# Gate columns of a fused decoder layer: two products per chunk instead of three, an added half on VectorE, softmax weights scaled on ScalarE

## The chip, the cores and the metric

One core of one Trainium2 chip. The time is the device time of one execution in microseconds; before the change it is 456.95 us, the median of three runs (456.88 to 457.21). Lower is better.

## The reference, cut to what matters

One decoder layer on 256 tokens of 1024 features, all in float32. A first half mixes tokens, a second half is a SwiGLU. The mixer, on its modulated and normalised input `h`:

```python
proj = h @ w_in                                   # 256 x 6504
(q_sb, k_sb, v_sb, q_mb, k_mb, v_mb, q_ds, k_ds, v_ds,
 q_ix, k_ix, w_ix, gate_logits) = jnp.split(proj, ...)
o_sb = stick_breaking_attention(q_sb, k_sb, v_sb)     # 6 heads, no softmax
o_mb = moba_attention(q_mb, k_mb, v_mb, slopes)       # 5 heads, softmax
o_ds = dsa_attention(q_ds, k_ds, v_ds, ...)           # 5 heads, softmax over 64 picked keys
g_sb, g_mb, g_ds = jnp.split(jax.nn.sigmoid(gate_logits + b_gate), 3, axis=-1)
merged = g_sb * (o_sb @ w_proj_sb) + g_mb * (o_mb @ w_proj_moba) + g_ds * (o_ds @ w_proj_dsa)
y = merged @ w_o
```

The 3 x 1024 columns of `gate_logits` are what the change touches, and beside them the division of the softmax weights by their sum in the ten softmax heads.

## The kernel before, in words

**Numbers in two parts.** A float32 operand of a matrix product is cut into a high part (`whi`, `hhi`) and the rest (`wlo`, `hlo`). ScalarE makes the high part by a copy (`cut_hi`, L749), VectorE the rest by a subtraction (`cut_lo`, L1113). TensorE then adds three products, high x high, high x low and low x high, in one PSUM bank (`three`, L1579 to L1581). The two parts of `h` lie side by side in `hcut` (128 partitions, 8 chunks, 2 parts, 256 tokens), so the two parts of a chunk are also one operand of 512 columns. The SwiGLU's first product already uses that (`up`, L1982 and L1983): one product of 512 columns with `whi`, which puts high x high in the first half of a bank and high x low in the second, and one of 256 columns with `wlo`, added to the second half.

**Units.** The product with `w_in` is made in 51 units, numbered 0 to 50, of up to 128 features for all tokens (or up to 384 features for 128 tokens). Weights come in blocks of up to 512 columns. The last 24 units, 27 to 50 (`FIRST_GATE` = 27), are the gate columns, four units to a block (blocks 11 to 16). Two banks take turns; `unit(u)` on TensorE (L1677) waits until the bank of unit u-2 has been read, and `take_unit(u)` on ScalarE (L800, gates in L829) reads it: it adds the bias and writes to `gates`, which has `qk`'s place, so the trace calls it qk. Up to unit 45 L829 adds the bias alone, and from 46 (`SIGMOID_FROM`) it makes the sigmoid too; in the passes of units 46 to 49 four larger instructions (L968) make the sigmoid of the 19 tiles before.

**One order for all engines.** Every engine runs through a pass for each u, and tables say what else a pass holds: `PIECES_AT` the cuts of the next block (a quarter each in the gate passes, two in the first pass of block 16), `SCORES_AT`, `EXP_AT`, `NORM_AT` and `SECOND_AT` the four steps of an attention head (head n begins in pass 14+2n, its steps in successive passes), `OUTPUT_AT` the product with the values, `ROUND_AT` one of eight rounds of the top-64 search, `ADA_AT` a step of a matrix-vector product on VectorE whose weights GpSimd's queue loads (`accumulate`, L1184). In a pass VectorE cuts first (L1113), then comes OUTPUT (L1330, which waits for ScalarE's L949), the step of NORM, that of EXP, that of SCORES, the round and the accumulations. ScalarE in a pass cuts (L749), makes a stick-breaking head's step of EXP (L914 to L916), takes the unit, makes the stick-breaking step of NORM (L921), the softmax EXP (L941), OUTPUT (L949) and the step of SECOND (L957, L960). TensorE in a pass makes the unit, then OUTPUT (L1768, L1770), SECOND (L1738 and L1739, or the transposes L1750) and SCORES.

For a softmax head VectorE takes 1/sum (L1337) and multiplies the weights by it, a 128x128 and a 128x256 part (L1339), in the pass of NORM. TensorE transposes the result at the end of the next pass. For a stick-breaking head VectorE adds in the pass of EXP (L1357), GpSimd masks (L707), ScalarE cuts (L921), VectorE makes the rest (L1344) in the pass of NORM, and TensorE's L1738 waits for it one pass later. Heads 0 to 4 and 11 to 15 are softmax heads, 5 to 10 stick-breaking.

**After the units.** Eight steps f of the merge: TensorE multiplies the heads' outputs with the projections (L1579 to L1581 with `ohi`, L1892, L1893), VectorE multiplies by the gates (L1409), adds (L1415, L1420) and cuts (L1425), and between these cuts the weights of the projections (L1113) and of `w_o` (L1119). ScalarE cuts high parts (L749, L763, L974). Then comes the product with `w_o` on TensorE, whose chunk 6 waits for VectorE's last L1119.

## Time and profile before

| | |
|---|---|
| median of three runs | 456.95 us |
| the profiled execution | 456.9 us, its span 455.2 us |
| granted TensorE clock | 0.996 of full speed |
| PE (TensorE) busy | 440.2 us, 97% |
| DVE (VectorE) busy | 330.7 us, 73% |
| ACT (ScalarE) busy | 243.6 us, 54% |
| POOL (GpSimd) busy | 35.1 us, 8% |
| gate units | from 122.7 to about 212.6 us of the span |

Between the time of an execution and its span lie 1.7 us ahead of and behind what the profile shows. Times in the rows are microseconds from the start of the span. A row of a timeline has the start, the length, the engine, the line, the operation, out<-in with shapes and, in brackets, the idle time of the engine before it with what ended it. Instructions of one engine overlap at their ends, so what one costs a busy engine is the distance from its start to the next one's, which is called its step here, and not its length.

### The profile page before, as it was taken

What the parts mean: (1) busy time and instruction counts of PE and PEld (TensorE: products, weight loads), DVE (VectorE), ACT (ScalarE), POOL (GpSimd) and SP (SyncE); (2) the same over time, 40 slices, a digit from 0 to 9 for tenths busy, and PEclk for the clock granted to TensorE, in tenths of its full rate; (3) what the DMA queues carried; (4) which work ended last, traced back from release to release, by engine and by line L of the source; (5) the groups of instructions that cost most, each with busy time, mean ns of one, the idle gap of its engine ahead of it and who ended that gap; (6) DMA issues with size and microseconds to landing.
All of it is one profiled execution on the core that took longest, in us unless ns stands there. A gap on an engine that the chain in (4) does not pass through costs nothing.

```text
span 455.2 us, 7884 instructions
## 1 busy us (share of the span) xinstructions
PE 440.2 (97%) x2966; PEld 388.9 (85%) x2966; DVE 330.7 (73%) x587; ACT 243.6 (54%) x432; POOL 35.1 (8%) x76
## 2 busy tenths in 40 slices
PE   5999999999999999999999999999999999999994
PEld 3678998999999899999997899888888888888883
DVE  4625659887898887866995785896696687677655
ACT  4413885565777755587554676443534525425332
POOL 2000102100322231000000001000000000000000
PEclk9999999999999999999999999999999999999998
DMA  8999376797688558745559516998748658530002
GB/s 291 383 377 341 115 257 200 278 303 261 233 286 308 157 185 313 237 140 194 181 224 351 203 49 194 371 314 268 234 157 291 201 184 275 185 138 0 1 0 92
DMA packets 61634, 99.86 MB, mean 219 GB/s; under 512 B 3892, under 2 KB 44452, under 8 KB 61604
## 3 DMA queue, kind: packets, MB, share of 16 engines
q1 hardware_dynamic: 56480, 81.57, 52.8%
q0 software_dynamic: 4960, 17.84, 11.2%
q8 instruction: 19, 0.31, 0.3%
q14 instruction: 11, 0.09, 0.1%
q10 hardware_dynamic: 164, 0.05, 0.0%
HBM read 98.40 MB, written 1.05 MB: 218 GB/s over the span
## 4 chain that ended last, share of the span: by engine, by line
PE 91%; DVE 4%; issue 2%; ACT 2%; DMA 1%; SPq 0%; DVEq 0%; ACTq 0%
PE psum L1579 17%; PE psum L1982 16%; PE psum L1580 16%; PE psum L1581 16%; PE psum L1983 8%; PE psum L1641 3%; PE psum L1929 3%; PE psum L1595 2%; PE psum L1768 1%; DVE wlo L1113 1%; DMA xt<-in_x_dram 1%; PE psum L1703 1%; PE psum L1701 1%; PE psum L1630 1%; PE psum L1750 1%
## 5 line engine op out<-in xcount | busy, mean ns | idle before, releaser
L1982 PE MATMUL psum<-hcut,whi 128*128 128x512 f32 x320 | 111.5, 392 | 0.0
L1983 PE MATMUL psum<-hcut,wlo 128*128 128x256 f32 x320 | 89.5, 280 | 0.0
L1579 PE MATMUL psum<-hcut,whi 128*128 128x256 f32 x280 | 82.1, 293 | 0.3 <-DVE wlo L1113 0.3
L1580 PE MATMUL psum<-hcut,whi 128*128 128x256 f32 x280 | 79.1, 283 | 0.0
L1581 PE MATMUL psum<-hcut,wlo 128*128 128x256 f32 x280 | 79.1, 282 | 0.0
L1113 DVE TENSOR_TENSOR wlo<-raw,whi 128x768 fp32r<-128x768 f32 (+3 forms) x68 | 64.4, 972 | 15.6 <-ACT whi L749 15.0
L1982 PEld LDWEIGHTS psum<-hcut,whi 128*128 128x128 f32 x320 | 59.9, 187 | 13.2
L1983 PEld LDWEIGHTS psum<-hcut,wlo 128*128 128x128 f32 x320 | 60.4, 189 | 0.3
L749 ACT ACTIVATE whi<-raw 128x768 fp32r<-128x768 f32 (+3 forms) x68 | 55.6, 850 | 6.4 <-PE psum L1893 3.2
L1579 PEld LDWEIGHTS psum<-hcut,whi 128*128 128x128 f32 x280 | 53.4, 191 | 5.5 <-ACT qk L829 1.8
L1580 PEld LDWEIGHTS psum<-hcut,whi 128*128 128x128 f32 x280 | 53.5, 191 | 0.0
L1581 PEld LDWEIGHTS psum<-hcut,wlo 128*128 128x128 f32 x280 | 53.5, 191 | 0.0
L1490 DVE TENSOR_TENSOR dlo<-draw,dhi 128x2048 fp32r<-128x2048 f32 x11 | 25.1, 2292 | 35.4 <-ACT dhi L1008 35.4
L1485 DVE TENSOR_TENSOR wlo<-raw,whi 128x1024 fp32r<-128x1024 f32 x36 | 42.4, 1220 | 3.0 <-ACT whi L1001 3.0
L1057 ACT ACTIVATE fsil<-fsil 128x256 f32<-128x256 f32 x20 | 8.4, 418 | 63.5 <-DVE fsil L1504 63.5
L1001 ACT ACTIVATE whi<-raw 128x1024 fp32r<-128x1024 f32 x36 | 35.9, 1045 | 0.0
L1580 PE MATMUL psum<-dlo,fhi 128*128 128x512 f32 x88 | 34.4, 391 | 0.0
L1579 PE MATMUL psum<-dhi,fhi 128*128 128x512 f32 x88 | 34.4, 391 | 0.0
L1581 PE MATMUL psum<-dhi,flo 128*128 128x512 f32 x88 | 34.2, 389 | 0.0
L1008 ACT ACTIVATE dhi<-draw 128x2048 fp32r<-128x2048 f32 x11 | 21.0, 1914 | 22.3 <-PE psum L1581 22.3
L1184 DVE SCALAR_TENSOR_TENSOR acc<-xn,csil,acc 128x1024 f32<-128x1024 f32 x21 | 26.9, 1281 | 4.2 <-DMA xn<-in_w_ada_dram 3.5
L1580 PE MATMUL psum<-wlo,hcut 128*128 128x320 f32 (+2 forms) x76 | 26.2, 345 | 0.0
(252 smaller groups left out, 830.8 us busy)
## 6 DMA issues: line engine op xcount, KB each, us to landing
raw<-in_w_up_dram SPq DMA_DIRECT2D x22, 1024.0 KB, 7.5
xn<-in_w_ada_dram POOLq DMA_DIRECT2D x32, 512.0 KB, 4.9
raw<-in_w_in_dram SPq DMA_DIRECT2D x6, 2048.0 KB, 8.9
draw<-in_w_down_dram SPq DMA_DIRECT2D x11, 1024.0 KB, 5.0
ada<-in_w_ada_dram SPq DMA_DIRECT2D x16, 384.0 KB, 9.3
raw<-in_w_in_dram SPq DMA_DIRECT2D x3, 1536.0 KB, 8.9
raw<-in_w_o_dram SPq DMA_DIRECT2D x8, 512.0 KB, 4.5
raw<-in_w_in_dram SPq DMA_DIRECT2D x3, 1280.0 KB, 7.2
```

Source lines behind the costliest of these rows:

```text
L749: act.activation(block_view(whi[b % 2], b)[0:p, chunks, cols], block_view(raw[b % 2], b)[0:p, chunks, cols], ACT.Copy).then_inc(w_hi, 1)
L1001: act.activation(block_view(whi[part], B_FFN)[:, 2 * q:2 * q + 2, :], block_view(raw[part], B_FFN)[:, 2 * q:2 * q + 2, :], ACT.Copy).then_ ...
L1008: act.activation(dhi[slot][:, :, :], draw[slot][:, :, :], ACT.Copy).then_inc(d_hi, 1)
L1113: dve.tensor_tensor(block_view(wlo[b % 2], b)[0:p, chunks, cols], block_view(raw[b % 2], b)[0:p, chunks, cols], block_view(whi[b % 2], b)[ ...
L1184: ins = dve.scalar_tensor_tensor(sums, part, csil[:, k:k + 1], sums, ALU.mult, ALU.add)
L1485: dve.tensor_tensor(block_view(wlo[part], B_FFN)[:, 2 * q:2 * q + 2, :], block_view(raw[part], B_FFN)[:, 2 * q:2 * q + 2, :], block_view(w ...
L1490: dve.tensor_tensor(dlo[slot][:, :, :], draw[slot][:, :, :], dhi[slot][:, :, :].bitcast(F32), ALU.subtract).then_inc(d_lo, 1)
L1579: pe.matmul(dst, a[0], b[0], start=first, stop=False)
L1580: pe.matmul(dst, a[0], b[1], start=False, stop=False)
L1581: return pe.matmul(dst, a[1], b[0], start=False, stop=last)
L1982: pe.matmul(dst[:, :], wh, hcut[:, k, :, :].rearrange("p a s -> p (a s)"), start=k == 0, stop=False)
L1983: mm = pe.matmul(dst[:, S:2 * S], wl, hhi[:, k, :], start=False, stop=k == KC - 1)
```

## The change

In a gate unit TensorE makes two products per chunk instead of three, one of 512 columns and one of 256. ScalarE's L829 adds the bias to the first half of the bank. VectorE then adds the second half to it in `gates` (`take_gate`, behind the cuts of its pass), and TensorE's gate unit u waits for that of unit u-2 in place of ScalarE's reading. From unit 46 on the sigmoid is no longer made in `take_unit`: five instructions behind the last pass make it (`late_gate`). In the softmax heads VectorE only takes 1/sum, and ScalarE multiplies the weights by it, behind OUTPUT in the same pass.

```diff
@@ semaphores
+        gate_read, sum_inverse = sem("gate_read"), sem("sum_inverse")
@@ ScalarE
+            def late_gate(u):
+
+                act.wait_ge(gate_read, u - FIRST_GATE + 1)
+                act.activation(gates[:, UNITS[u][4], :], gates[:, UNITS[u][4], :], ACT.Sigmoid).then_inc(sig_ready, 1)
+
...
-                    ins = act.activation(gates[:, dest, :], src[:, 0:S], ACT.Sigmoid if u >= SIGMOID_FROM else ACT.Identity,
+                    ins = act.activation(gates[:, dest, :], src[:, 0:S], ACT.Identity,
                                          bias=vecs[:, VEC_GATE + dest:VEC_GATE + dest + 1])
...
+                if u in NORM_AT and NORM_AT[u] in SOFT_NO:
+                    n = NORM_AT[u]
+                    act.wait_ge(sum_inverse, SOFT_NO[n] + 1)
+                    for t, (c0, c1) in enumerate(((0, P), (P, CAUSAL))):
+                        ins = act.activation(bufp[n % 2][:, c0:c1], bufp[n % 2][:, c0:c1], ACT.Copy, scale=ssum[:, n % 2, t:t + 1])
+                    ins.then_inc(p_ready, 1)
...
-                        act.wait_ge(unit_read, SIGMOID_FROM)
+                        act.wait_ge(gate_read, EARLY_GATES)
                     tiles = slice(EARLY_GATES * i // SIGMOID_BATCHES, EARLY_GATES * (i + 1) // SIGMOID_BATCHES)
                     act.activation(gates[:, tiles, :], gates[:, tiles, :], ACT.Sigmoid).then_inc(sig_ready, 1)
+            for u in range(SIGMOID_FROM, N_UNITS):
+                late_gate(u)
@@ VectorE
+            def take_gate(u):
+
+                g, src = UNITS[u][4], bank[B_UNIT + u % 2]
+                dve.wait_ge(unit_read, u + 1)
+                dve.tensor_tensor(gates[:, g, :], src[:, S:2 * S], gates[:, g, :], ALU.add).then_inc(gate_read, 1)
+
...
+                if u >= FIRST_GATE:
+                    take_gate(u)
...
-                    then(dve.reciprocal(ssum[:, n % 2, :], ssum[:, n % 2, :]))
-                    for t, (c0, c1) in enumerate(((0, P), (P, CAUSAL))):
-                        ins = dve.tensor_scalar(bufp[n % 2][:, c0:c1], bufp[n % 2][:, c0:c1], ssum[:, n % 2, t:t + 1], None, ALU.mult)
-                    ins.then_inc(p_ready, 1)
+                    dve.reciprocal(ssum[:, n % 2, :], ssum[:, n % 2, :]).then_inc(sum_inverse, 1)
...
-                    dve.wait_ge(sig_ready, SIGMOID_BATCHES)
-                    dve.wait_ge(unit_read, N_UNITS)
+                    dve.wait_ge(sig_ready, SIGMOID_BATCHES + N_UNITS - SIGMOID_FROM)
@@ TensorE
                 if u < FIRST_UNIT + 2:
                     pe.wait_ge(unit_read, 2 * (u - FIRST_UNIT + 1))
+                elif u < FIRST_GATE + 2:
+                    pe.wait_ge(unit_read, u - 1)
                 else:
-                    pe.wait_ge(unit_read, u - 1)
+                    pe.wait_ge(gate_read, u - 2 - FIRST_GATE + 1)
...
-                    if what != "values":
+                    if what == "gate":
+                        pe.matmul(bank[B_UNIT + u % 2][:, :], w[0][:, k, :], hcut[:, k, :, :].rearrange("p a s -> p (a s)"),
+                                  start=k == 0, stop=False)
+                        mm = pe.matmul(bank[B_UNIT + u % 2][:, S:2 * S], w[1][:, k, :], hhi[:, k, :], start=False, stop=k == KC - 1)
+                    elif what != "values":
...
-                    pe.wait_ge(unit_read, N_UNITS)
+                    pe.wait_ge(gate_read, N_UNITS - FIRST_GATE)
```

## Rows read from the trace of the kernel before

**Rows 1.** The page's first part: busy time of each engine.
```profile
PE 440.2 (97%) x2966; PEld 388.9 (85%) x2966; DVE 330.7 (73%) x587; ACT 243.6 (54%) x432; POOL 35.1 (8%) x76
```

**Rows 2.** Busy time by stretch: PE, PEld, DVE, ACT, POOL, PEclk, DMA share, GB/s.
```profile
127.00:157.00 30.00, 30.00 (x246) 27.59 (x245) 26.17 (x50) 21.40 (x39) 7.73 (x22) 1.00 0.74 251
213.00:245.00 32.00, 31.05 (x230) 28.91 (x229) 31.30 (x54) 17.74 (x29) 0.00 (x0) 1.00 0.67 231
198.57:213.21 14.64, 14.64 (x115) 13.17 (x114) 8.74 (x14) 11.56 (x19) 1.05 (x2) 1.00 0.64 200
```

**Rows 3.** Timeline of VectorE in the merge, its first and last cuts.
```profile
214.56 2.16 DVE L1113 TENSOR_TENSOR wlo<-raw,whi 128x768 fp32r<-128x768 f32 x3
...
243.48 1.22 DVE L1119 TENSOR_TENSOR wlo<-raw,whi 128x1024 fp32r<-128x1024 f32 x1
```

**Rows 4.** Timeline of TensorE where chunk 6 of the product with w_o begins.
```profile
244.80 0.47 PE L1579 MATMUL psum<-whi,hcut 128*128 128x512 f32 x1 [0.54 <-issue]
```

**Rows 5.** Timeline of TensorE in unit 29, chunks 0 and 7 of the second product.
```profile
131.78 0.28 PE L1580 MATMUL psum<-hcut,whi 128*128 128x256 f32 x1
...
134.29 0.28 PE L1580 MATMUL psum<-hcut,whi 128*128 128x256 f32 x1
```

**Rows 6.** Timeline of TensorE in the SwiGLU, first and last of 26 products, every second one.
```profile
277.04 0.40 PE L1982 MATMUL psum<-hcut,whi 128*128 128x512 f32 x1
...
285.71 0.39 PE L1982 MATMUL psum<-hcut,whi 128*128 128x512 f32 x1
```

**Rows 7.** Timeline of TensorE: unit 27, before its chunk 6.
```profile
125.41 0.36 PE L1579 MATMUL psum<-hcut,whi 128*128 128x256 f32 x1 [0.29 <-DVE wlo L1113]
```

**Rows 8.** Timeline of VectorE, passes 24 to 34: pieces around the added work.
```profile
115.58 0.55 DVE L1339 TENSOR_SCALAR bufp<-bufp,ssum 128x128 f32<-128x128 f32 x2
116.05 0.61 DVE L1384 MAX8 top<-work 128x8 f32<-128x128 f32 x2
...
139.55 0.43 DVE L1330 TENSOR_TENSOR olo<-psum,ohi 128x256 fp32r<-128x256 f32 x1 [1.11 <-ACT ohi L949]
139.90 0.55 DVE L1344 TENSOR_TENSOR sp_lo<-bufp,sp_hi 128x384 fp32r<-128x384 f32 x1
...
150.44 1.28 DVE L1184 SCALAR_TENSOR_TENSOR acc<-xn,csil,acc 128x1024 f32<-128x1024 f32 x1 [1.33 <-DMA xn<-in_w_ada_dram]
...
156.15 0.55 DVE L1344 TENSOR_TENSOR sp_lo<-bufp,sp_hi 128x384 fp32r<-128x384 f32 x1
```

**Rows 9.** Timeline of VectorE in pass 35: the late L1357.
```profile
161.36 0.55 DVE L1357 SCALAR_TENSOR_TENSOR bufp<-psum,bufa 128x384 f32<-128x384 f32 x1
```

**Rows 10.** Timeline of TensorE: head 9's second step, and the start of unit 37.
```profile
157.48 0.34 PE L1738 MATMUL psum<-sp_hi,tri 128*128 128x384 f32 x1
...
162.30 0.39 PE L1579 MATMUL psum<-hcut,whi 128*128 128x256 f32 x1
```

**Rows 11.** Timeline of GpSimd: head 10's mask.
```profile
161.98 1.46 POOL L707 TENSOR_SCALAR_AFFINE_SELECT bufp<-bufp 128x128 f32<-128x128 f32 x2 [2.24 <-DVE bufp L1357]
```

**Rows 12.** Timeline of ScalarE, step of EXP in pass 25.
```profile
120.50 0.53 ACT L916 ACTIVATE bufa<-bufa 128x384 f32<-128x384 f32 x1
```

**Rows 13.** Timeline of ScalarE, passes 46 to 50 and the merge.
```profile
196.90 1.28 ACT L829 ACT_TABLE_LOAD   x1
...
198.57 0.38 ACT L949 ACTIVATE ohi<-psum 128x256 fp32r<-128x256 f32 x1
198.83 1.06 ACT L968 ACTIVATE qk<-qk 128x1024 f32<-128x1024 f32 x1
...
212.83 0.48 ACT L829 ACTIVATE qk<-psum,vecs 128x256 f32<-128x256 f32 x1 [0.58 <-PE psum L1581]
213.21 2.39 ACT L749 ACTIVATE whi<-raw 128x768 fp32r<-128x768 f32 x4
...
220.06 0.40 ACT L974 ACTIVATE hcut<-xn 128x256 fp32r<-128x256 f32 x1
220.36 1.14 ACT L749 ACTIVATE whi<-raw 128x512 fp32r<-128x512 f32 x2
```

## The prediction

> **What bounds the kernel now.** I read the page's busy times first. TensorE is busy for 97% of the span, VectorE for 73%, ScalarE for 54% [rows 1]. Time taken off TensorE is thus worth having unless another engine sets the pace where it is taken, and the table by stretch shows two such places. From 127 to 157 us, in the first gate units, VectorE is busy for 26.17 of 30 us. From 213 to 245 us, in the merge, it is busy for 31.30 of 32 us and TensorE for 31.05 [rows 2]. In the merge VectorE's timeline has no gap between its first cut at 214.56 and the end of its last at 244.70 [rows 3], and TensorE stands still for 0.54 us and begins chunk 6 at 244.80, right behind that last cut [rows 4]. So the mixer ends when VectorE's chain through the merge ends. All that follows hangs on this, loads and the second half of the layer included, and moves with it. **The change is worth what it does to the start of that chain at 214.56.** TensorE's gain in the gate units counts only as far as it gets there.
>
> **TensorE's products.** The second product of a gate unit starts at 131.78 in chunk 0 and at 134.29 in chunk 7 [rows 5]. That is 2.51 us for seven chunks, 0.3586 us for three products. The pair of the new form stands in the SwiGLU, with the same shapes and operands: 25 pairs lie between 277.04 and 285.71 [rows 6], 0.3468 us each. A chunk saves 0.0118 us, a unit of eight 0.094 us. The columns that move are the same, 768 either way; only an instruction and its weight load go. Unit 27 gains nothing, since its chunk 6 waits at 125.41 for VectorE's cut [rows 7]. So 23 units give 23 x 0.094 = 2.17 us at most. Both stretches ran at a granted clock of 1.00 [rows 2].
>
> The row gives 119.5 ns for a product of 256 columns. A rule in the Trainium skill speaks against the change here: "TensorE: Matmul & The Clock Gate", section "Back-to-back issue gap", has a gap of columns over 2.4 GHz plus about 2.5 ns, so that a pair would save only those 2.5 ns, an estimated 0.5 us over the units. Its 109 ns for 256 columns is not what this trace shows.
>
> **VectorE's additions.** 24 additions of a 128x256 half in PSUM to SBUF. The nearest row has the same size and one operand in PSUM: L1330, 0.43 us long, with the next instruction 0.35 us after its start [rows 8]. I take 0.35, with 0.43 as the upper bound, and 24 x 0.35 = 8.4 us in all. Taken away are ten pairs of L1339, of 0.47 us a pair (115.58 to 116.05) [rows 8], but only five of these lie in gate passes, and none in passes 27 to 37, where the heads are stick-breaking ones. The five ahead of the gates bring nothing by themselves: the one in pass 24 lets VectorE come 0.47 us earlier to L1357, but that waits for ScalarE's L916, which ends at 121.03 [rows 12], so unit 27 starts no earlier.
>
> **Where that hurts.** The bank waits are easy at first: the addition of u-2 has all of unit u-1 to be made in. The lag is what counts. I follow VectorE from pass 28. Its idle time of 1.11 us before 139.55 takes up three additions, and the wait for a loaded weight row before 150.44 takes up the next two, if the load lands when it did [rows 8]. From there it has no idle time. The additions of 33 and 34 make head 9's L1344 start at 156.15 + 0.70 = 156.85, and end at 157.4. TensorE wants it behind unit 35, at 157.48 before [rows 10], less eight gains of 0.094, that is at 156.73. **It waits about 0.7 us and has lost what it had gained.** In pass 35 L1357, at 161.36 before [rows 9], is preceded by a third addition and comes at 161.36 + 3 x 0.35 = 162.4. Unit 37, which started at 162.30 [rows 10], needs that addition: another 0.15. Behind L1357 come GpSimd's mask of 1.46 us [rows 11], ScalarE's cut and VectorE's rest, so head 10's L1738 is late too, by some 0.35 us. TensorE's units 36 and 37 gained 0.19, the stalls come to 1.3 us in all, and it stands about 0.4 us behind its time before. From pass 38 on VectorE is relieved of an L1339 every second pass and the stalls end. Units 38 to 50 give 13 x 0.094 = 1.2 us, and unit 50 ends about 0.8 us earlier.
>
> **ScalarE.** The scaling of a softmax head's weights is two instructions. ScalarE's 256-column copy in SBUF has a step of 0.30 us (220.06 to 220.36), and the one with a bias column 0.38 (212.83 to 213.21) [rows 13]. I take 0.7 us for both, between 0.5 and 0.85. It also waits for VectorE's reciprocal, with the next cut queued behind it. Until pass 45 its idle time covers this: over 127 to 157 it is busy for 21.40 of 30 us [rows 2]. If it doesn't, the next block's cut comes late, and TensorE with it.
>
> Pass 46 has no such cover. Before, the table load at 196.90 ran while ScalarE waited for unit 46. Now it comes behind OUTPUT and the scaling, then the first sigmoid, 1.06 us long at 198.83 before [rows 13]. ScalarE did 11.56 us of work between 198.57 and 213.21 [rows 2]. It now begins about 0.55 us earlier, at 198.0 (TensorE's lead in pass 46: 9 x 0.094 less the 0.4, with rounding), and has 11.56 + 1.28 + 0.7 + 0.3 for the reciprocal = 13.84 us, so it is through at 211.85. That is close to TensorE's unit 50, which it reads at 212.83 - 0.84 = 212.0. I take 212.0.
>
> **The tail.** Behind that reading (0.38 us) come five late sigmoids at the copy's step of 0.30 us (bounds 0.30 and its length, 0.40), and then the cuts for the merge: four in 2.39 us, the first, the widest, about 0.85 [rows 13]. VectorE's chain can start at 212.0 + 0.38 + 1.5 + 0.85 = 214.7, against 214.56. **Sum:** -2.17 of TensorE's, +1.3 of stalls in units 35 to 37, +1.0 of tail (214.7 less 214.56, less the -0.84 of unit 50): +0.15 us. Against the profiled execution's 456.9 that is 457.05, and the median of the runs is 456.95, 0.05 above it. I predict 457.0.
>
> **Rivals.**
> - *VectorE keeps up* (0.26). The stalls don't come, because the weight rows land earlier or VectorE's steps pack more densely. Unit 50 is read at 212.83 - 2.17 = 210.7, and ScalarE's queue, begun 1.8 us earlier, ends at 210.6. The chain starts at 213.4, that is -1.15: 455.8. For it speaks that VectorE has 3.8 us idle in the 30 [rows 2]. Against it, much of this idle time is before instructions that wait for other engines.
> - *The lag grows* (0.24), and this is slower. Its place is passes 33 to 37. Weight rows are loaded when the one before is used up, and compete with the blocks, whose loads wait for VectorE's cuts. If the row of 150.44 lands 0.8 us later or more, every step above is later by as much, and TensorE ends its units at the time of before or 0.3 us later. With the tail unchanged that is +1.0 to +1.3: 458.1. It decides from about 0.7 us of further lag.
> - *The pair is no faster* (0.08). If a pair in the gate units costs as much as three products, the gain is 0 to 0.5 us, VectorE's lag hides behind TensorE, and the tail remains: 457.7. The SwiGLU's rows speak against it. The skill's rule above would give this case.
> - The forecast has 0.42.
>
> **Range and chances.** A measurement of this kernel tells about 0.2%, 0.9 us, from no change. The forecast's own range is 456.2 to 457.8 (sigmoids of 0.40 add 0.5, a scaling of 0.5 and shorter stalls take off as much). To hold 8 in 10 the range goes to the middle of both main rivals: 455.7 to 458.2. Faster is nearly all of the first rival and a little of the forecast, 0.27. Slower is the second and edges of the forecast and the third, 0.31. That leaves 0.42.
>
> **What would show it.** Pairs at 0.347 us in the gate units. A wait of L1738 for VectorE of about 0.7 us near 157 us, and TensorE's idle time there instead of none. L968's table load behind the scaling in pass 46. ScalarE without a gap up to unit 50. The first L1113 of the merge at 214.7 and no gap behind it up to the last L1119. If the merge's chain starts early and the time doesn't follow, or if VectorE is no longer gapless there, then what I call the bound is wrong.

## The result and the profile after

| | kernel before | changed kernel |
|---|---|---|
| median of 8 runs each | 457.07 us (456.48 to 457.58) | 458.61 us (458.05 to 459.04) |
| the profiled execution, its span | 456.9 us, 455.2 us | 458.74 us, 457.0 us |
| granted TensorE clock | 0.996 | 0.998 |

The ratio is 1.0031 with a 95% interval of 1.0020 to 1.0042. The change costs 1.5 us, 0.3% of the time. The forecast was 457.0 in a range of 455.7 to 458.2, so the result lies 0.4 us above the range, and on the side to which 0.31 was given. One execution of the kernel before, among those run beside kernels 5 to 8 below, took 1106 us and is left out of all numbers here.

The page's first part for the changed kernel, against [rows 1]:

```profile
PE 439.7 (96%) x2774; PEld 377.5 (83%) x2774; DVE 333.4 (73%) x591; ACT 252.4 (55%) x457; POOL 34.6 (8%) x76
```

TensorE has 192 instructions fewer and is busy for 0.5 us less, VectorE for 2.7 us more, ScalarE for 8.8 us more. Three stretches of the changed kernel, in the columns of [rows 2]:

```profile
127.00:157.00 30.00, 30.00 (x187) 24.30 (x186) 28.52 (x57) 21.82 (x40) 7.93 (x22) 1.00 0.75 257
213.00:245.00 32.00, 30.20 (x227) 28.25 (x227) 30.58 (x54) 19.17 (x33) 0.14 (x1) 1.00 0.69 231
198.57:213.21 14.64, 14.64 (x84) 11.63 (x85) 9.33 (x16) 13.34 (x20) 1.05 (x2) 1.00 0.51 162
```

In the first gate units VectorE went from 26.17 to 28.52 us of 30, and TensorE still never stands still. In the last, ScalarE went from 11.56 to 13.34 us of 14.64.

**A common zero.** Parts that the change doesn't touch drift between executions: unit 27 starts at 122.69 before and at 123.03 here, unit 10 is read at 62.84 and 63.20. So below, times count from the start of unit 27 where executions are compared. That this is fair shows in the fourteen profiled executions of this document: from the reading of unit 10 to the start of unit 27 all take 59.8 to 60.0 us, with the softmax scaling on either engine, and from the start of the merge chain's last cut to the end of the span 211.7 to 211.9 us. What differs lies ahead of the reading of unit 10, which comes between 61.67 and 63.20, and between unit 27 and that last cut. Units 27 to 50, start to start, took 86.97 us before (122.69 to 209.66) and 86.75 now (123.03 to 209.78). **TensorE gained 0.22 us net, where the forecast had 0.8.** Its timeline in the changed kernel, with the pairs of units 29 and 35 and the stalls behind them (TensorE, then its weight loads):

```profile
132.26 0.40 PE L1710 MATMUL psum<-hcut,whi 128*128 128x512 f32 x1
...
134.34 0.40 PE L1710 MATMUL psum<-hcut,whi 128*128 128x512 f32 x1
...
154.85 0.40 PE L1710 MATMUL psum<-hcut,whi 128*128 128x512 f32 x1
...
156.97 0.40 PE L1710 MATMUL psum<-hcut,whi 128*128 128x512 f32 x1
157.34 0.45 PE L1762 MATMUL psum<-sp_hi,tri 128*128 128x384 f32 x1
...
180.39 0.55 PE L1774 MATMUL psum<-ident,bufp 128*128 128x128 f32 x3 [0.24 <-ACT bufp L960]
```
```profile
157.34 0.19 PEld L1762 LDWEIGHTS psum<-sp_hi,tri 128*128 128x128 f32 x1 [0.18 <-DVE sp_lo L1363]
...
160.95 0.42 PEld L1678 LDWEIGHTS psum<-ident,mrow 128*128 128x128 f32 x4 [0.31 <-DVE mrow L1204]
...
162.42 0.19 PEld L1710 LDWEIGHTS psum<-hcut,whi 128*128 128x128 f32 x1 [0.36 <-DVE qk L1314]
...
165.56 0.19 PEld L1762 LDWEIGHTS psum<-sp_hi,tri 128*128 128x128 f32 x1 [0.41 <-DVE sp_lo L1363]
...
180.38 0.31 PEld L1774 LDWEIGHTS psum<-ident,bufp 128*128 128x128 f32 x3 [0.57 <-ACT bufp L960]
```

Six pairs of unit 29 take 2.08 us, 0.3467 each, as forecast. Six of unit 35 take 2.12, 0.3533. Of the 23 units from 28 on, eight are like unit 29 (2.07 to 2.09 us) and fifteen like unit 35 (2.11 or 2.12), while six triples take 2.15 or 2.16 us in every one of these units before. And the weight loads, which run ahead of the products, wait five times between 157 and 181 us: for VectorE's rest of a stick-breaking head (L1363), for its copy L1204, for its addition L1314, and for ScalarE's scaling L960. VectorE at its last weight row ahead of these waits, then ahead of the third and fourth of them, and VectorE and ScalarE ahead of the fifth:

```profile
150.36 1.28 DVE L1198 SCALAR_TENSOR_TENSOR acc<-xn,csil,acc 128x1024 f32<-128x1024 f32 x1 [0.25 <-DMA xn<-in_w_ada_dram]
...
160.21 0.69 DVE L1204 COPY mrow<-psum 128x512 f32<-128x512 f32 x1
160.82 1.22 DVE L1127 TENSOR_TENSOR wlo<-raw,whi 128x1024 fp32r<-128x1024 f32 x1
161.95 0.42 DVE L1314 TENSOR_TENSOR qk<-psum,qk 128x256 f32<-128x256 f32 x1
162.28 0.55 DVE L1376 SCALAR_TENSOR_TENSOR bufp<-psum,bufa 128x384 f32<-128x384 f32 x1
162.75 1.22 DVE L1127 TENSOR_TENSOR wlo<-raw,whi 128x1024 fp32r<-128x1024 f32 x1
163.88 0.42 DVE L1314 TENSOR_TENSOR qk<-psum,qk 128x256 f32<-128x256 f32 x1
164.95 0.56 DVE L1363 TENSOR_TENSOR sp_lo<-bufp,sp_hi 128x384 fp32r<-128x384 f32 x1 [0.65 <-ACT sp_hi L927]
...
179.01 0.42 DVE L1314 TENSOR_TENSOR qk<-psum,qk 128x256 f32<-128x256 f32 x1
179.34 0.15 DVE L1359 RECIPROCAL ssum<-ssum 128x2 f32<-128x2 f32 x1
```
```profile
179.53 0.80 ACT L960 ACTIVATE bufp<-bufp,ssum 128x128 f32<-128x128 f32 x2 [2.68 <-DVE ssum L1359]
```

The weight row that held VectorE up before 150.44 in the kernel before [rows 8] lets it go on at 150.36 here, 150.02 less the drift of 0.34, so it landed 0.42 us earlier. An addition has a step of 0.33 us (161.95 to 162.28). VectorE is without a gap from 154.93 to 164.3, and unit 37 can't start before its addition of unit 35 has ended at 162.37. At 179.34 the reciprocal comes behind a cut and an addition, and ScalarE, idle for 2.68 us, scales only then.

ScalarE and VectorE at the end of the gate units, against [rows 3, 13], and the load of block 19 (blocks 17 to 20 hold the projections of the heads' outputs) on SP's queue:

```profile
199.64 0.80 ACT L960 ACTIVATE bufp<-bufp,ssum 128x128 f32<-128x128 f32 x2 [0.63 <-DVE ssum L1359]
200.47 1.28 ACT L980 ACT_TABLE_LOAD   x1
201.76 1.06 ACT L980 ACTIVATE qk<-qk 128x1024 f32<-128x1024 f32 x1
202.72 1.35 ACT L750 ACTIVATE whi<-raw 128x768 fp32r<-128x768 f32 x2
203.98 0.46 ACT L835 ACTIVATE qk<-psum,vecs 128x256 f32<-128x256 f32 x1
...
212.91 0.48 ACT L835 ACTIVATE qk<-psum,vecs 128x256 f32<-128x256 f32 x1 [0.53 <-PE psum L1712]
213.29 1.63 ACT L804 ACTIVATE qk<-qk 128x256 f32<-128x256 f32 x5
214.82 2.39 ACT L750 ACTIVATE whi<-raw 128x768 fp32r<-128x768 f32 x4
220.47 1.37 ACT L750 ACTIVATE whi<-raw 128x768 fp32r<-128x768 f32 x2 [3.25 <-DMA raw<-in_w_proj_dsa_dram]
```
```profile
209.20 0.68 DVE L1127 TENSOR_TENSOR wlo<-raw,whi 64x512 fp32r<-64x512 f32 x1
...
215.69 2.16 DVE L1127 TENSOR_TENSOR wlo<-raw,whi 128x768 fp32r<-128x768 f32 x3 [0.67 <-ACT whi L750]
...
221.34 1.56 DVE L1127 TENSOR_TENSOR wlo<-raw,whi 128x768 fp32r<-128x768 f32 x2 [0.37 <-ACT whi L750]
...
245.06 1.22 DVE L1133 TENSOR_TENSOR wlo<-raw,whi 128x1024 fp32r<-128x1024 f32 x1
```
```profile
209.95 0.37 SPq L578 DMA_DIRECT2D raw<-in_w_proj_sb_dram  x1
```

The same two points in the kernel before, on VectorE and on SP's queue:

```profile
207.30 0.69 DVE L1113 TENSOR_TENSOR wlo<-raw,whi 64x512 fp32r<-64x512 f32 x1
```
```profile
208.06 0.37 SPq L577 DMA_DIRECT2D raw<-in_w_proj_sb_dram  x1
```

In pass 46 reciprocal, scaling, table load and sigmoid stand in one row, so ScalarE's reading of unit 47 comes at 203.98, 2.7 us later than before (201.28). The cuts of block 17 slip with it. Its last, which frees the buffer for block 19, is at 209.20 instead of 207.30, and the load goes out at 209.95 instead of 208.06. At the end the five late sigmoids take 1.53 us ahead of the four cuts. The merge chain starts at 215.69, 92.66 us after unit 27 (before 91.87): +0.8. Then it waits 0.37 us for block 19, where before it had no gap, and its last cut comes at 122.03 us after unit 27 (before 120.79): +1.24. TensorE's chunk 6 follows [rows 4]:

```profile
246.38 0.47 PE L1597 MATMUL psum<-whi,hcut 128*128 128x512 f32 x1 [0.53 <-issue]
```

It starts at 246.38 instead of 244.80, later by 1.58, of which 0.34 were there at unit 27.

### The profile page after: what moved, and what is told of

Its sections match the earlier page's. It is cut to its first block, busy times and chain, and to the rows that moved or that the text cites. A ratio compares the mean times of both kernels' runs of the same rounds, so it can differ in the third digit from the quotient of the medians.

```text
span 457.0 us, 7529 instructions
## 1 busy us (share of the span) xinstructions
PE 439.7 (96%) x2774; PEld 377.5 (83%) x2774; DVE 333.4 (73%) x591; ACT 252.4 (55%) x457; POOL 34.6 (8%) x76
## 4 chain that ended last, share of the span: by engine, by line
PE 78%; DVE 10%; issue 4%; ACT 3%; DMA 3%; POOL 1%; DVEq 0%; SPq 0%; ACTq 0%
PE psum L2006 16%; PE psum L1597 11%; PE psum L1598 11%; PE psum L1599 11%; PE psum L2007 8%; PE psum L1659 4%; PE psum L1710 4%; PE psum L1953 3%; PE psum L1613 2%; DVE acc L1198 2%; DVE wlo L1127 2%; PE psum L1712 2%; DMA xn<-in_w_ada_dram 1%; DMA xt<-in_x_dram 1%; POOL bufp L708 1%
## 5 line engine op out<-in xcount | busy, mean ns | idle before, releaser
L2006 PE MATMUL psum<-hcut,whi 128*128 128x512 f32 x320 | 111.7, 392 | 0.0
L2007 PE MATMUL psum<-hcut,wlo 128*128 128x256 f32 x320 | 89.6, 280 | 0.0
L1710 PE MATMUL psum<-hcut,whi 128*128 128x512 f32 x192 | 70.7, 407 | 0.3 <-DVE wlo L1127 0.3
L2006 PEld LDWEIGHTS psum<-hcut,whi 128*128 128x128 f32 x320 | 59.9, 187 | 13.3
L2007 PEld LDWEIGHTS psum<-hcut,wlo 128*128 128x128 f32 x320 | 60.5, 189 | 0.3
L1712 PE MATMUL psum<-hcut,wlo 128*128 128x256 f32 x192 | 53.7, 280 | 0.0
L1710 PEld LDWEIGHTS psum<-hcut,whi 128*128 128x128 f32 x192 | 36.0, 188 | 11.4 <-issue 2.5
L1712 PEld LDWEIGHTS psum<-hcut,wlo 128*128 128x128 f32 x192 | 36.3, 189 | 0.0
L1597 PE MATMUL psum<-hcut,whi 128*128 128x256 f32 x88 | 25.7, 293 | 0.0
L1598 PE MATMUL psum<-hcut,whi 128*128 128x256 f32 x88 | 24.9, 283 | 0.0
```

Source lines behind the costliest of these rows:

```text
L1597: pe.matmul(dst, a[0], b[0], start=first, stop=False)
L1598: pe.matmul(dst, a[0], b[1], start=False, stop=False)
L1710: pe.matmul(bank[B_UNIT + u % 2][:, :], w[0][:, k, :], hcut[:, k, :, :].rearrange("p a s -> p (a s)"), start=k == 0, stop=False)
L1712: mm = pe.matmul(bank[B_UNIT + u % 2][:, S:2 * S], w[1][:, k, :], hhi[:, k, :], start=False, stop=k == KC - 1)
L2006: pe.matmul(dst[:, :], wh, hcut[:, k, :, :].rearrange("p a s -> p (a s)"), start=k == 0, stop=False)
L2007: mm = pe.matmul(dst[:, S:2 * S], wl, hhi[:, k, :], start=False, stop=k == KC - 1)
```

## The experiments

Twelve kernels ran, five rounds each, with runs of the kernel before between them on the same chip. They form five batches (1 to 4, 5 to 8, 9 and 10, 11, 12), and the changed kernel ran in none of them, so across batches it is the ratios to the kernel before that compare, not the medians. Kernel 2 has six runs, the others 11 or 12. The diffs show the lines that matter; `...` stands for the rest. Ahead of each result stands what the theories expected of it. A: the loss lies at the end of the gate units, in ScalarE's pass 46 and the five late sigmoids. B: VectorE's additions and the split softmax division stall TensorE among passes 36 to 46 and eat what the pairs give. C: VectorE is short of time in general. The letters D, F, G and H came up on the way and are told where they are used, D first in kernel 5: the arrival of block 19's columns bounds the merge. "After unit 10" counts from ScalarE's reading of that unit.

**1. The softmax scaling back on VectorE** (changed kernel)

```diff
-  dve.reciprocal(ssum[:, n % 2, :], ssum[:, n % 2, :]).then_inc(sum_inverse, 1)
+  then(dve.reciprocal(ssum[:, n % 2, :], ssum[:, n % 2, :]))
+  for t, (c0, c1) in enumerate(((0, P), (P, CAUSAL))):
+      ins = dve.tensor_scalar(bufp[n % 2][:, c0:c1], bufp[n % 2][:, c0:c1], ssum[:, n % 2, t:t + 1], None, ALU.mult)
+  ins.then_inc(p_ready, 1)
...
```

The dots are ScalarE's scaling, which is taken out.

> The changed kernel with the softmax weights scaled on VectorE again, all else of the change kept. Against 458.6 us of the changed kernel. Theory A (the loss sits at the end of the gate units: ScalarE's queue from pass 46 with the table load behind the scaling, and the five late sigmoids): unit 41's wait for L960 goes, the queue of pass 46 begins its table load about 1.1 us earlier, but the late sigmoids remain: about 458.1. Theory B (the loss is the coupling of VectorE and ScalarE through the reciprocal in the softmax passes 38 to 46): about 457.4. Theory C (VectorE is short of time, and every us given back to it costs): slower, about 459.2.

Measured: 457.87 us, ratio to before 1.0016 (1.0004 to 1.0028). The stall of unit 41 is gone, another of 0.32 us for `smax` stands ahead of unit 40, and units 27 to 50 take 86.86 us, no less than in the changed kernel: in the units the stall has only moved. What this execution gains is behind them, where the merge chain no longer waits for block 19 and its last cut comes 0.27 us earlier against unit 27. More work on VectorE made the kernel no slower, rather faster, which speaks against C.

**2. The four merge cuts ahead of the late sigmoids** (changed kernel)

```diff
+ for b, q in MERGE_PIECES[0]:
+     cut_hi(B_PROJ + b, q)
  for u in range(SIGMOID_FROM, N_UNITS):
      late_gate(u)
...
```

> The changed kernel with ScalarE's four cuts for the merge ahead of the five late sigmoids instead of behind them. Theory A: VectorE's first cut of the merge starts 0.7 us earlier, and the multiplication by the gates waits for the sigmoids instead, some 0.3 us: about 458.1 us. Theories B and C: what ScalarE does behind unit 50 doesn't matter, 458.6.

Measured: 458.47 us, 1.0042 (1.0030 to 1.0055), no gain. From the start of unit 50 the first cut came 0.67 us earlier than in the changed kernel (5.24 us behind it instead of 5.91), which is A's 0.7. Against unit 27 it came only 0.24 us earlier, since in this execution TensorE's weight loads waited for the scaling L960 a second time, in unit 43 (0.72 us). And the chain then waited 0.71 us for block 19, and its last cut was 0.25 us later than in the changed kernel. So the new order gives what it should where it stands, and the next waits take it back.

**3. The table loaded before unit 46 is read** (changed kernel)

```diff
+ if u == SIGMOID_FROM:
+     act.activation(warm[:, :], csil[:, 0:1], ACT.Sigmoid)
  take_unit(u)
```

> The changed kernel with a sigmoid of one column ahead of the reading of unit 46, so that the table is loaded while ScalarE waits for TensorE, as it was before the change. Theory A: block 17 is cut 1.2 us earlier, the load of block 19 is issued earlier by as much, and VectorE's wait of 0.37 us near 221 us and TensorE's near it go; unit 50 is no earlier: about 458.0 us. Theories B and C: 458.6.

Measured: 457.53 us, 1.0015 (1.0003 to 1.0027). The table load at 196.41 now lies in ScalarE's wait for unit 46, unit 47 is read at 202.09, and the merge chain has no gap. The first cut is as late as in the changed kernel (92.71 after unit 27), the last 0.4 us earlier (121.63). ScalarE still waited 2.40 us for block 19's load, but no longer too long for VectorE.

**4. The pairs alone** (kernel before). TensorE makes pairs, and the second half of the bank is never added to the gates, so the product of the low activations is left out.

```diff
- if what != "values":
+ if what == "gate":
+     pe.matmul(bank[B_UNIT + u % 2][:, :], w[0][:, k, :], hcut[:, k, :, :].rearrange("p a s -> p (a s)"),
+               start=k == 0, stop=False)
+     mm = pe.matmul(bank[B_UNIT + u % 2][:, S:2 * S], w[1][:, k, :], hhi[:, k, :], start=False, stop=k == KC - 1)
+ elif what != "values":
```

> The kernel before with the pairs of products alone: ScalarE reads the first half of the bank as before and nobody adds the second, so the gates lack high x low and low x high. It shows what TensorE's gain is worth with nothing else changed. If the units' gain (1.4 to 2.2 us) reaches the start of VectorE's chain through the merge: 455.3 to 455.9 us. If ScalarE's queue in passes 46 to 50 holds the chain's start where it was: 456.5 or more, against 457.07 of the kernel before.

Measured: 455.53 us, 0.9974 (0.9965 to 0.9984). TensorE at the start of units 27 and 50:

```profile
122.83 0.39 PE L1690 MATMUL psum<-hcut,whi 128*128 128x512 f32 x1
...
208.52 0.50 PE L1690 MATMUL psum<-hcut,whi 128*128 128x512 f32 x1
```

That is 85.69 us against 86.97: **the pairs give 1.28 us, and the median falls by 1.3.** So over the runs, what TensorE gains in the gate units does get to the end. In VectorE's timeline a second bound shows right behind the first:

```profile
213.44 2.16 DVE L1113 TENSOR_TENSOR wlo<-raw,whi 128x768 fp32r<-128x768 f32 x3
...
219.54 1.56 DVE L1113 TENSOR_TENSOR wlo<-raw,whi 128x768 fp32r<-128x768 f32 x2 [0.82 <-ACT whi L749]
```

The chain starts 1.26 us earlier against unit 27 and then waits 0.82 for block 19. Its last cut comes 120.44 us after unit 27, only 0.35 us earlier than before. This profiled execution, at 456.93 us, was the longest of the kernel's twelve.

**5. Pairs and additions in units 27 to 45 only** (changed kernel, scaling on VectorE)

```diff
- if what == "gate":
+ if what == "gate" and u < SIGMOID_FROM:
- if u >= FIRST_GATE:
+ if FIRST_GATE <= u < SIGMOID_FROM:
      take_gate(u)
- ins = act.activation(gates[:, dest, :], src[:, 0:S], ACT.Identity,
+ ins = act.activation(gates[:, dest, :], src[:, 0:S], ACT.Sigmoid if u >= SIGMOID_FROM else ACT.Identity,
- for u in range(SIGMOID_FROM, N_UNITS):
-     late_gate(u)
...
```

> The changed kernel, but the last five gate units (46 to 50) have the three products and the direct sigmoid of the kernel before, and VectorE scales the softmax weights again. So the pairs and VectorE's additions stay in units 27 to 45, and no late sigmoid stands ahead of the four cuts of the merge. Theory A (the loss is at the end of the gate units: the table load behind the reading of unit 46 and the five late sigmoids): the first merge cut starts some 1.9 us after that of the table-early run less 0.9, that is about 151.2 to 151.5 us after unit 10 is read (before 151.7, changed 152.5), the last cut 0.5 to 1.2 us earlier than in the changed kernel (181.9 after that read), and the median is 456.0 to 456.7. Theory B (VectorE's additions among passes 27 to 46 cost as much as the pairs give): 457.3 to 457.9, since the additions are all but five still there. Theory D (the arrival of block 19's columns bounds the merge as soon as the cuts come earlier): the first cut comes earlier as under A, but ScalarE's cuts L750 of that block wait for the DMA, and the median is 456.5 to 457.2.

Measured: 456.96 us, 1.0003 (0.9991 to 1.0014), between what A and B expected. It is the time that D expected, but not D's way: no cut of the merge waits for a load in this execution. The last cut comes 1.36 us earlier than in the changed kernel, against unit 27. But units 27 to 50 take 86.85 us, 1.16 more than with the pairs alone. 0.2 of that are the last five units' own gain. The rest are stalls: unit 37 lasts 3.14 us instead of 2.92 in kernel 4, and ahead of unit 40 TensorE waits for VectorE:

```profile
172.44 0.52 PE L1770 MATMUL psum<-ident,bufp 128*128 128x128 f32 x3 [0.37 <-DVE smax L1388]
```

**6. The same with the scaling on ScalarE** (the edit of 1 left out)

> As the last-five-old run, with the scaling of the softmax weights on ScalarE as in the changed kernel. Theory A: ScalarE's queue around pass 46 is no longer behind (the table load stands at the reading of unit 46 again), so it is within 0.3 us of the last-five-old run. Theory B: the coupling of reciprocal and scaling costs 0.4 to 0.7 us more than the last-five-old run, as it did between the changed kernel and the one with the scaling back.

Measured: 457.45 us, 1.0012 (0.9999 to 1.0024). The median is 0.5 us above kernel 5's, as B expected, but within the two intervals. TensorE waits for L960 at 179.28 (0.26 us) and 186.78 (0.32), units 27 to 50 take 87.47 us. The wait for `smax` ahead of unit 40 is gone.

**7. The scaling on ScalarE alone** (kernel before, the scaling's part of the change)

> The kernel before with one part of the change alone: ScalarE scales the softmax weights, VectorE only takes the reciprocal. Theory B: the step itself costs 0.4 to 0.8 us, 457.3 to 457.7. Theory A: without the additions on VectorE the reciprocal comes early and the scaling is hidden; the table load at the reading of unit 46 is delayed by at most the 0.8 of the scaling: within 0.3 us of the kernel before. Theory C (VectorE is short of time): 0.3 to 0.6 us faster.

Measured: 456.89 us, 1.0001 (0.9987 to 1.0015), units 27 to 50 in 86.91 us. From unit 28 to 50 no product of TensorE waits for another engine, as A expected: without additions the scaling is hidden. Freeing VectorE of it brings nothing either, again not as C has it.

**8. The late sigmoids alone** (kernel before)

```diff
- ins = act.activation(gates[:, dest, :], src[:, 0:S], ACT.Sigmoid if u >= SIGMOID_FROM else ACT.Identity,
+ ins = act.activation(gates[:, dest, :], src[:, 0:S], ACT.Identity,
+ for u in range(SIGMOID_FROM, N_UNITS):
+     act.wait_ge(unit_read, u + 1)
+     act.activation(gates[:, UNITS[u][4], :], gates[:, UNITS[u][4], :], ACT.Sigmoid).then_inc(sig_ready, 1)
...
```

> The kernel before with the late sigmoids alone: ScalarE reads units 46 to 50 with bias and without the sigmoid, the table load comes at the batch of sigmoids of pass 46, and five sigmoids of 128 x 256 stand ahead of the four cuts of the merge. No pairs, no additions. Theory A: the first merge cut 1.2 to 1.6 us later than before (151.7 us after unit 10 is read), block 17's last cut and with it the load of block 19 later by up to 1 us, and the median 457.8 to 458.3, 1.0 to 1.5 us over the kernel before. Theory B: the five sigmoids cost at most 0.5 us, 456.9 to 457.3.

Measured: 457.90 us, 1.0019 (1.0010 to 1.0028), in A's range. ScalarE and VectorE at the start of the merge:

```profile
212.39 1.64 ACT L803 ACTIVATE qk<-qk 128x256 f32<-128x256 f32 x5
213.93 2.40 ACT L749 ACTIVATE whi<-raw 128x768 fp32r<-128x768 f32 x4
```
```profile
214.80 2.16 DVE L1120 TENSOR_TENSOR wlo<-raw,whi 128x768 fp32r<-128x768 f32 x3 [1.06 <-ACT whi L749]
```

The first cut comes 93.05 us after unit 27 instead of 91.87, 1.2 us later, with no pairs and no additions in the kernel.

**9. Kernel 5 with the addition behind the softmax steps of its pass.** Theory F: it is the place of the addition that stalls TensorE. G: it is the amount of work. The addition moves from behind the cuts to behind the step of SCORES.

```diff
- if FIRST_GATE <= u < SIGMOID_FROM:
-     take_gate(u)
...
+ if FIRST_GATE <= u < SIGMOID_FROM:
+     take_gate(u)
  if u in ROUND_AT:
```

> The last-five-old kernel (pairs and additions in units 27 to 45, three products and the direct sigmoid in units 46 to 50, scaling on VectorE) with the addition of each pass moved behind VectorE's softmax steps of that pass. In the last-five-old run the pairs gave 0.058 us a unit, but units 35 to 40 with what stands between them took 0.9 to 1.0 us more than in the run without additions (unit 37 lasted 3.14 instead of 2.92, the stretch between units 39 and 40 0.91 instead of 0.36). Theory F (the place: the addition of 0.42 stands ahead of the steps that TensorE waits for): most of those 0.9 go, unit 50 starts about 86.0 us after unit 27 starts (last-five-old 86.85, before 86.97, pairs without additions 85.69), and the median is 455.8 to 456.4. Theory G (the amount: VectorE is without a gap from 157 to 173 us, and what an addition no longer delays another step does): unit 50 starts 86.6 to 87.0 after unit 27, and the median is 456.7 to 457.2.

Measured: 457.25 us, 1.0006 (0.9996 to 1.0015), units 27 to 50 in 87.86 us, a full us more than in kernel 5. F fell, and G too had unit 50 too early. TensorE now waits for the copy and for the addition itself, which comes late enough to hold up the unit after next:

```profile
160.56 0.66 PE L1675 MATMUL psum<-ident,mrow 128*128 128x128 f32 x4 [0.33 <-DVE mrow L1196]
...
162.49 0.50 PE L1707 MATMUL psum<-hcut,whi 128*128 128x512 f32 x1 [0.42 <-DVE qk L1306]
```

**10. Kernel 5 with pairs and additions in units 27 to 34 and 41 to 45 only.** H: VectorE carries a debt over from the passes before.

```diff
+ PAIRED = [*range(27, 35), *range(41, 46)]
...
- if what == "gate" and u < SIGMOID_FROM:
+ if what == "gate" and u in PAIRED:
...
```

> The last-five-old kernel with pairs and additions only in units 27 to 34 and 41 to 45; units 35 to 40 have the three products of the kernel before and no addition. Theories F and G agree that the stalls of units 35 to 40 go with their additions: 13 pairs by 0.058 are 0.75, unit 50 starts 86.2 to 86.3 us after unit 27, and the median is 456.1 to 456.5. If instead the additions of passes 27 to 34 make VectorE late for passes 35 to 40 (theory H: a debt that VectorE carries over), part of the stalls stays, unit 50 starts 86.5 to 86.9 after unit 27, and the median is 456.7 to 457.0.

Measured: 457.06 us, 0.9999 (0.9984 to 1.0013). Units 27 to 50 took 86.61 us, which is in H's range. Against the kernel before, unit 36 lasts 0.12 us longer and unit 38 0.28 longer, and there TensorE waited 0.25 for GpSimd's mask L701. But that doesn't show H's debt: kernel 8, which has no additions and up to unit 45 nothing changed, waits for the same mask in unit 38, by 0.27 us in its weight loads. H is not shown. In the merge this execution waited 1.11 us for block 20 (VectorE):

```profile
226.31 1.56 DVE L1121 TENSOR_TENSOR wlo<-raw,whi 128x768 fp32r<-128x768 f32 x2 [1.11 <-ACT whi L751]
```

The runs spread from 455.74 to 459.01 us. Whether this form beats the kernel before by less than the interval's 0.16% is not settled.

**11. The changed kernel without the additions.** All 24 are left out, TensorE and the sigmoids wait for ScalarE's reading alone, and the product of the low activations is not in the gates.

```diff
- if u >= FIRST_GATE:
-     take_gate(u)
- pe.wait_ge(gate_read, u - 2 - FIRST_GATE + 1)
+ pe.wait_ge(unit_read, u - 1)
- act.wait_ge(gate_read, u - FIRST_GATE + 1)
+ act.wait_ge(unit_read, u + 1)
...
```

> The changed kernel with VectorE's 24 additions left out: TensorE and the sigmoids wait for ScalarE's reading alone, and the product of the low activations never reaches a gate. The pairs, the scaling on ScalarE, the place of the table load and the five late sigmoids stay. If the parts add up as measured one by one (pairs without additions -1.3 us against the kernel before, scaling on ScalarE alone -0.1 or nothing, late sigmoids alone +0.8 to +0.9), the median is 456.3 to 456.7, and the additions with what they delay are worth 1.9 to 2.3 us of the changed kernel's time (458.6). The stalls of units 35 to 41 go (unit 50 starts 85.6 to 85.8 us after unit 27; changed kernel 86.75), and the first merge cut comes 151.7 to 151.9 us after unit 10 is read. The rival (the late sigmoids are the whole loss): the median is 457.8 to 458.4, hardly faster than the changed kernel.

Measured: 456.91 us, 1.0002 (0.9987 to 1.0017). Units 27 to 50 take 85.66 us, as in kernel 4. So the late sigmoids aren't the whole loss. The additions with what they delay are worth 1.3 us by the two ratios (1.0031 and 1.0002) and 1.7 us by the two medians, which come from different batches. The parts taken one by one had 456.3 to 456.7 us, so the sum is 0.2 us or more too low. Half of the twelve runs lie at 456.35 to 456.80, the others at 457.03 to 458.72. What held the profiled one up, of 458.50, shows on ScalarE, VectorE and SP's queue; the others have no trace:

```profile
220.26 1.37 ACT L750 ACTIVATE whi<-raw 128x768 fp32r<-128x768 f32 x2 [4.21 <-DMA raw<-in_w_proj_dsa_dram]
```
```profile
214.51 2.16 DVE L1127 TENSOR_TENSOR wlo<-raw,whi 128x768 fp32r<-128x768 f32 x3 [1.01 <-ACT whi L750]
...
221.14 1.56 DVE L1127 TENSOR_TENSOR wlo<-raw,whi 128x768 fp32r<-128x768 f32 x2 [1.34 <-ACT whi L750]
```
```profile
208.78 0.37 SPq L578 DMA_DIRECT2D raw<-in_w_proj_sb_dram  x1
```

The chain starts 0.3 us earlier than before against unit 27, and loses 1.34 us to block 19, whose load went out at 208.78.

**12. Kernel 11 with the last piece of block 17 cut one pass earlier.** D: the load of block 19, let go by that cut, is a bound of its own.

```diff
...
  PIECES_AT = pieces_at()
+ PIECES_AT[48] += PIECES_AT.pop(49)
```

> The change without additions once more, with the last piece of block 17 cut in pass 48 instead of pass 49, so that its buffer is free and the load of block 19 is issued earlier (208.8 us in the run before this one, where unit 10 is read at 63.06; there the merge chain waited 1.34 us for that block). Theory D (half of the executions of the run without additions end some 1.5 us late because block 19's columns arrive after ScalarE wants them): the load is issued 0.8 to 2 us earlier, no cut of the merge waits for it, and the median falls to 456.2 to 456.6 with few executions above 457.5. Against D (the late executions have another cause, or another load takes its place): the median stays at 456.7 to 457.2 and the runs spread as widely as before.

Measured: 457.04 us, 1.0003 (0.9994 to 1.0012). The load goes out at 206.91, 84.55 us after unit 27 instead of 85.84. No cut of the merge waits for it, and no run is above 457.67. But the earlier cut stands ahead of VectorE's copy L1205, and TensorE waits for that in unit 49:

```profile
207.49 0.66 PE L1677 MATMUL psum<-ident,mrow 128*128 128x128 f32 x4 [0.60 <-DVE mrow L1205]
```

The long runs went as D expected. The median did not fall as D expected, and where six runs of kernel 11 lie at 456.80 or below, here two do, for which the 0.60 us in unit 49 may be the reason.

**All together.** Units 27 to 50 start to start, and the first and last cut of VectorE's merge chain, both from the start of unit 27, in us of one profiled execution each. The ratios are of 6 to 12 runs of each kernel. One execution isn't the median: those of kernels 2 and 8 were the shortest of their runs, that of kernel 4 the longest, and that of kernel 11 is one of the long half. So the last cut and the ratio don't go in step.

| kernel | 27 to 50 | first cut | last cut | ratio to before |
|---|---|---|---|---|
| before | 86.97 | 91.87 | 120.79 | 1 |
| changed | 86.75 | 92.66 | 122.03 | 1.0031 |
| 1 scaling on VectorE | 86.86 | 92.76 | 121.76 | 1.0016 |
| 2 merge cuts first | 87.18 | 92.42 | 122.28 | 1.0042 |
| 3 table early | 86.81 | 92.71 | 121.63 | 1.0015 |
| 4 pairs alone | 85.69 | 90.61 | 120.44 | 0.9974 |
| 5 last five old | 86.85 | 91.76 | 120.67 | 1.0003 |
| 6 as 5, ScalarE scales | 87.47 | 92.38 | 121.56 | 1.0012 |
| 7 ScalarE scales, alone | 86.91 | 91.82 | 121.07 | 1.0001 |
| 8 late sigmoids alone | 87.09 | 93.05 | 121.97 | 1.0019 |
| 9 as 5, addition later | 87.86 | 92.77 | 121.69 | 1.0006 |
| 10 as 5, fewer pairs | 86.61 | 91.52 | 121.64 | 0.9999 |
| 11 no additions | 85.66 | 91.57 | 121.90 | 1.0002 |
| 12 as 11, cut earlier | 86.51 | 92.37 | 121.27 | 1.0003 |

## Why the prediction was wrong

**The frame held.** The mixer ends with VectorE's merge chain. In all fourteen profiled executions the rest of the span behind its last cut is the same within 0.25 us, whatever the kernel, and TensorE's chunk 6 starts 1.3 us after the start of that cut. When the chain's start moved alone (kernels 4 and 8) the median followed by -1.3 and +0.8 us. What the frame lacked is that the chain can also be held in its middle, by the load of block 19. Kernel 4 waits 0.82 us there, kernel 11 1.34, the changed kernel 0.37.

**The pair's gain was mis-sized.** "A chunk saves 0.0118 us, a unit of eight 0.094 us", 2.17 us in all. The triple's step was the same in every unit, but the pair's came from the SwiGLU alone. It holds in eight of the changed kernel's 23 units from 28 on. In the other fifteen a pair costs 0.3533 us, which saves less than half as much. Kernel 4 measures 1.28 us from unit 27 to unit 50, 0.058 for each of the 22 units 28 to 49, where the forecast has 2.07: **0.8 us less gain.** It is still more than twice the estimated 0.5 us of the rule in the Trainium skill, "TensorE: Matmul & The Clock Gate", section "Back-to-back issue gap", by which only 2.5 ns per product left out are saved. The page gives that formula for a single product by itself, and this trace agrees with neither its 109 ns for 256 columns nor its saving: it has 119.5 ns before and 7 ns saved per pair.

**The stalls came out near in size by luck: little more than half of them were where they were forecast.** Forecast were 1.3 us in units 35 to 37 (their parts, 0.7, 0.15 and 0.35, add to 1.2), with 0.7 of them at L1738 near 157 us. Measured are 1.1 (86.75 less 85.66 of kernel 11): 0.12, 0.23 and 0.32 in units 35, 36 and 37, and 0.46 in unit 41, of which the forecast had nothing. The 0.7 came as a wait of 0.18 because VectorE's L1363 started at 156.74, 156.40 less the drift of 0.34, instead of the forecast 156.85. Of these 0.45 us, 0.42 are the weight row that landed earlier, where the prediction had set "if the load lands when it did". TensorE came to it 0.1 us later than forecast. The cause of the stall in unit 41 was named in the prediction ("It also waits for VectorE's reciprocal") and then costed at nothing, covered by ScalarE's idle time until pass 45. ScalarE was indeed idle, for 2.68 us, but with nothing to do: **idle time ahead of a late operand is no cover.** With the scaling back on VectorE (kernels 1 and 5), TensorE loses some 0.5 us ahead of unit 40 instead, so between units 27 and 50 the changed kernel loses nothing by the move, while kernel 6, with two such waits, takes 0.6 us more there than kernel 5. The scaling costs nothing without the additions (kernel 7). With them, kernels 1 and 5 are faster than the same with the scaling on ScalarE by 0.7 and 0.5 us, differences within their intervals; that the wait for it stalls TensorE is shown by the traces of the changed kernel and of kernel 6.

**The tail's own working was right, its start wasn't.** From the reading of unit 50 to the first cut the forecast had 2.7 us, the trace has 2.78 (212.91 to 215.69), with 1.53 for the five sigmoids. But unit 50 was to be read 0.84 us earlier than before and was read 0.26 earlier (212.91 less 0.34 against 212.83). So the chain starts 0.8 us late and not 0.14. That lead was missing because of the pairs and the stalls. Kernel 8 gives the late sigmoids a price by themselves: 1.2 us at the first cut, 0.8 at the median.

**Pass 46 was followed only to unit 50.** The prediction summed ScalarE's work, 13.84 us, and found it through in time, as it was (0.53 us idle ahead of 212.91). What it didn't follow is what those cuts release on the way: block 17's last cut 1.9 us later, hence the load of block 19 1.9 us later (1.6 against unit 27), hence a hole of 0.37 us in a chain for which the prediction had "no gap". With the table load moved forward (kernel 3) or the scaling taken away (kernel 1) that hole is gone, and the time with it by 0.7 us or more, though not by more than the two intervals together. The table load itself took 1.28 us with the sigmoid 1.29 us behind its start. The Trainium skill's "ScalarE: Activation LUTs", section "What ACT_TABLE_LOAD costs", has the same 1283 ns and some 1380 ns of draining besides; that drain is not in this trace, where the load starts 0.03 us behind the scaling's end.

**The sum as measured**, against unit 27: pairs -1.3, stalls +1.1, tail from unit 50 to the first cut +1.0 (92.66 less 86.75 is 5.91, before 4.90), the chain itself +0.45 with block 19's 0.37 in it: +1.24 at the last cut, where the forecast had +0.15. So of the 1.1 us that the forecast missed, 0.8 are the pairs and 0.45 the chain; the stalls, 0.2 less than forecast, took off a little, and the tail was right to 0.1. The two profiled executions differ by 1.8 us, with 0.34 ahead of unit 27 and 0.2 behind the last cut beside the 1.24. The medians differ by 1.5; how these divide among the places no trace tells.

**The rivals.** "VectorE keeps up" fell, since VectorE didn't, though its premise came in part: the weight row landed earlier. "The lag grows" had the sign and, with 458.1, the nearest size, but by luck: its row landed 0.42 us earlier instead of 0.8 later. "The pair is no faster" had part of it, and its 457.7 was nearer than the forecast.

**Open.** Why pairs of the same shapes differ by 2% from unit to unit wasn't tried. Nor was what makes block 19 arrive 10.3 to 11.7 us after its first issue in the seven executions in which ScalarE waited for it (changed kernel 209.95 to 220.47, kernel 4 207.01 to 218.66). Nor is it shown that the late block 19 costs the median anything: it held up single executions, and kernel 12, which loads it earlier, has no long runs, but its median is no lower. None of the nine forms that compute the whole gates beats the kernel before by what can be measured.

## What to carry to other kernels

An instruction taken from the bound engine is worth what it saves on average over the units, read from several of them, and what the busiest neighbour must do in exchange can spend it: here 24 additions of 0.33 us, in a queue that has no gap over long stretches, gave back 1.1 of 1.3 us in the units, and putting them later in the pass (kernel 9) made it worse. Work postponed past a loop stands in front of the next stage's first step: of the 1.5 us of late sigmoids in kernel 8, 1.2 show at the first cut. When a queue is lengthened, follow each of its instructions to the buffer it frees and the load that waits for that buffer, not only to the last one's end.

## What was unexpected of the hardware

- The same pair of products has a step of 0.3467 us in units 29 and 36 and 0.3533 in unit 35, all at a granted clock of 1.00. Three products of 256 columns take 0.358 to 0.360 us in every unit from 28 to 50.
- A hidden transfer became a bound by being issued 0.5 us (kernel 11) to 1.6 us (changed kernel) later against unit 27. The same load, wanted earlier in kernel 4, showed a wait though it was issued 1.2 us earlier than before. In kernel 10 the next block's was late: there two issues on SP's queue took 3.35 us, where they take 1.12 in the other executions:

```profile
218.14 3.35 SPq L584 DMA_DIRECT2D raw<-in_w_proj_moba_dram  x2
```

- Runs of one kernel on one chip spread by up to 3.5 us (kernel 7, 456.10 to 459.60; kernel 10, 455.74 to 459.01), while others keep within 1.5 (kernels 8 and 12). In the profiled executions 1.5 us of it lie ahead of the reading of unit 10, as much as the change costs. The spans of two single traces alone would have told little.
